# Joining the two 256-column products of a projection into one 512-column product

## The reference

```python
def swiglu(h, w_in, w_out):                       # w_in 1024 x 5632, w_out 2816 x 1024
    a, b = jnp.split(h @ w_in, 2, axis=-1)
    return (jax.nn.silu(a) * b) @ w_out

# first block, per layer: hx and hc are normalised x and ctx
q, k, v, ga, uf, gf, zc, bc, cc, gc = split_cols(hx @ w_in, PROJ_SIZES)   # 2816 columns
...                                               # the same w_in for hc; attention, Fourier, convolution
y = gated_merge(a, ga, f, gf, s, gc, w_out)       # ends in h @ w_out, 1024 x 1024

# second block, per layer: the same weights are applied to x and to hctx
x = x + 0.5 * mx[:, 2] * swiglu(ada_norm(x, ...), ffn_w_in[l, 0], ffn_w_out[l, 0])
hctx = hctx + 0.5 * mc[2] * swiglu(ada_norm(hctx, ...), ffn_w_in[l, 0], ffn_w_out[l, 0])
...                                               # mixer, then a second feed-forward network
```

## Time and profile before

| what | value |
|---|---|
| median of 3 runs (lowest, highest) | 2312.89 us (2312.33, 2319.12) |
| the profiled execution, first to last instruction | 2314.2 us |
| PE busy in it | 2227.1 us, 96% |
| DVE, ACT, POOL busy | 49%, 37%, 8% |
| mean granted PE clock | 0.987 of full speed |
| DMA, mean | 136 GB/s |

### The profile page before, as it was taken

One profiled execution on the slowest core, in us unless ns is written; L12 is line 12 of the kernel. 1 busy time (PEld: TensorE's weight loads), 2 busy tenths in 40 slices (PEclk: granted clock), 3 DMA queues, 4 the chain that ended last, 5 costly groups with the idle time before them and its releaser, 6 DMA issues. The chain is left out here.

```text
span 2314.2 us, 46991 instructions
## 1 busy us (share of the span) xinstructions
PE 2227.1 (96%) x19320; PEld 2091.2 (90%) x19320; DVE 1145.4 (49%) x1930; ACT 846.8 (37%) x1384; POOL 176.3 (8%) x150
## 2 busy tenths in 40 slices
PE   6999999899999999998999999999999999999998
PEld 5986798799999999976999999999999998979998
DVE  5227375653433445456653333454343446487665
ACT  4226454632221233248432222243232234455444
POOL 0003112100000010501200000010000010001000
PEclk9999999999999999999999999999999999999999
DMA  9853544445676244520354666242233233225573
GB/s 297 234 167 86 172 133 104 128 147 154 186 216 186 86 131 117 149 80 28 102 175 141 190 207 189 84 126 85 81 114 94 86 96 101 74 82 146 168 202 112
DMA packets 515900, 315.76 MB, mean 136 GB/s; under 512 B 16035, under 2 KB 513274, under 8 KB 515622
## 3 DMA queue, kind: packets, MB, share of 16 engines
q1 hardware_dynamic: 515160, 313.45, 46.1%
q10 hardware_dynamic: 590, 0.16, 0.0%
HBM read 312.50 MB, written 1.06 MB: 135 GB/s over the span
## 5 line engine op out<-in xcount | busy, mean ns | idle before, releaser
L1118 PE MATMUL ps<-h_hi,w_hi 128*128 128x256 f32 x3376 | 728.0, 280 | 3.5 <-DVE h_lo L1726 1.7
L1118 PE MATMUL ps<-h_lo,w_hi 128*128 128x256 f32 x3376 | 720.6, 278 | 0.0
L1118 PE MATMUL ps<-h_hi,w_lo 128*128 128x256 f32 x3376 | 720.6, 278 | 0.0
L1118 PEld LDWEIGHTS ps<-h_hi,w_hi 128*128 128x128 f32 x3376 | 537.8, 189 | 22.9 <-issue 21.6
L1118 PEld LDWEIGHTS ps<-h_lo,w_hi 128*128 128x128 f32 x3376 | 539.4, 189 | 0.1
L1118 PEld LDWEIGHTS ps<-h_hi,w_lo 128*128 128x128 f32 x3376 | 537.9, 189 | 0.0
L1960 DVE TENSOR_TENSOR w_lo<-stage,w_hi 128x1024 fp32r<-128x1024 f32 x227 | 285.0, 1258 | 441.5 <-ACT w_hi L1467 440.9
L1467 ACT ACTIVATE w_hi<-stage 128x1024 fp32r<-128x1024 f32 x227 | 236.6, 1055 | 334.4 <-PE ps L1118 200.4
L1960 DVE TENSOR_TENSOR w_lo<-deep,w_hi 128x1024 fp32r<-128x1024 f32 x184 | 226.1, 1234 | 226.9 <-ACT w_hi L1467 225.2
L1467 ACT ACTIVATE w_hi<-deep 128x1024 fp32r<-128x1024 f32 x184 | 191.9, 1055 | 179.7 <-PE ps L1118 141.4
L1118 PE MATMUL ps<-g_hi,w_hi 128*128 128x256 f32 x1100 | 232.9, 280 | 0.2
(11 more groups left out here) (413 smaller groups left out, 2858.0 us busy)
## 6 DMA issues: line engine op xcount, KB each, us to landing
modw<-in_ada_w SPq DMA_DIRECT2D x72, 1024.0 KB, 6.7
stage<-in_ffn_w_in SPq DMA_DIRECT2D x88, 512.0 KB, 3.9
deep<-in_ffn_w_in SPq DMA_DIRECT2D x88, 512.0 KB, 3.9
modw<-in_w_mod SPq DMA_DIRECT2D x18, 1024.0 KB, 6.1
stage<-in_w_in SPq DMA_DIRECT2D x30, 512.0 KB, 5.3
stage<-in_ffn_w_out SPq DMA_DIRECT2D x32, 384.0 KB, 3.5
stage<-in_even_w_in SPq DMA_DIRECT2D x24, 512.0 KB, 4.0
deep<-in_ffn_w_out SPq DMA_DIRECT2D x32, 384.0 KB, 3.4
```

Of the source, the lines that this page charges most:

```text
L1118: last = mm(ps[:, j, v - a:v - a + SEQ], w_part[wp][:, u % RING, c, :], x_part[xp][:, x, v:v + SEQ], start=first and wp == xp and v == a, ...
```

## The change

`chunk` no longer loops over the halves. Each of the three products of a chunk takes all columns `a` to `b` in one call: 512 columns where both halves of the tokens are in the projection, and 256 as before where only the latent ones are. Tiles, waits, signals and all other engines' programs stay as they are.

```diff
             def chunk(j, u, c, x, first, final):
                 for wp, xp in W_X:
-                    for v in range(a, b, SEQ):
-                        last = mm(ps[:, j, v - a:v - a + SEQ], w_part[wp][:, u % RING, c, :], x_part[xp][:, x, v:v + SEQ],
-                                  start=first and wp == xp and v == a, stop=final and wp == "lo", skip_group_check=True)
+                    last = mm(ps[:, j, 0:b - a], w_part[wp][:, u % RING, c, :], x_part[xp][:, x, a:b],
+                              start=first and wp == xp, stop=final and wp == "lo", skip_group_check=True)
                 return last
```

## The result

The changed kernel takes 2333.68 us (median of four runs, 2332.49 to 2334.57) against 2312.61 us for the kernel before on the same chip (2310.88 to 2319.12). The ratio is 1.0089, with a 95% interval from 1.0072 to 1.0106. The forecast of 2303.3 us was wrong in its sign, and the time lies outside its range. It is the time of the rival "the slow pace everywhere", 2333 us.

A forecast was written before the change was run, and what follows sets the result against it. PE's own pace was taken to bound the projections. Slow pairs saving 11 us, less 2 us for unsettled starts, plus 0.6 us for saved loads, gave 9.6 us off 2312.9: 2303.3 us, range 2297 to 2326 us.

The forecast's parts named there:

- the slow pace everywhere: Rival: unsettled 232 ns is the rule for joined products; 24 us lost, 4 gained, 2333 us; chance 0.19.
- The bound: In the projections only PE's own pace sets the end; PE is in flight for 2227.1 of 2314.2 us.
- The counts: 10788 general products of 256 columns form 5394 pairs; 5394 weight loads and 5394 starts of products go away.
- the hidden load: Weight load of 0.19 us runs beside the product before it; taking it away gives nothing by itself.
- The pace of the joined product: General products of 512 columns settle at 226.5 ns, as in the gate product; two quick halves take 226.6.
- The sum for the quick pace: About 1190 slow pairs save 11 us, unsettled starts cost 2, fewer loads at starts save 0.6: 9.6 us less.
- The mixed paces: Rival: joined products fall into quick or slow pace by stage; at 22% slow 2310 us; chance 0.23.
- The prediction's own test: Three stages of 396 products should fall from 46.96 to about 45.2 us, the 864-product projection stay at 98.
- The fixed cost per product: Rival: long projections reach 215.8 ns per 512-column product, 69 us less, 2244 us; chance 0.06.

The follow-up runs named there:

- e10: Changed kernel, weight ring moved 56 bytes on (distance 120), last network's activations 32 bytes on (distance 88): 2315.74 us, ratio 1.0010 to the kernel before.
- e9: Kernel before, still with halves of 256 columns, its weight ring moved 24 bytes on (distance 88): 2324.80 us, ratio 1.0052 to the kernel before.
- e1_streams: Small kernel of product streams alone, operand places varied from the changed kernel's addresses: 233.4 ns per 512-column product there, 226.6 with activations 64 bytes on.
- e5: Changed kernel with 192 unused bytes behind vtok, which makes the distance 0: 2324.92 us, ratio 1.0032 to the kernel before.
- e7_fine: Small kernel of product streams alone, distances in steps of 8 bytes, some 4, plus mixed kinds: 512 columns 226.7 ns at distance 120.
- e4_scan: Small kernel of product streams alone, distances 0 to 480 in steps of 32 bytes: joined products 226.6 ns at 0 and 256, 233.4 at 64.

## Why the prediction was wrong

**The bound, right.** PE's own pace sets the end, no wait grew, and the span followed the sums of the general products in each kernel of the table, up to the 5 to 10 us that everything else takes more once the layout is another.

**The counts, right; the hidden load, right at the quick pace.** 5394 products and loads went away, as counted. At their quick paces a joined product takes as long as two halves (97.98 us for 432 in e10, for 864 in e9), so that the saved loads and starts give nothing there, as the earlier trace rows let expect. Where the halves are slow, at the distances 0 and 128, joining takes 66.9 and 28.3 us off the 512-token stages; whether the load or the start that is saved does it was not separated.

**The pace of the joined product: the step that failed.** "With 128 weight columns, the very form that the change makes, ... it settles: 17 starts ..., 226.5 ns each." It is the same form only by the numbers of its shape. The gate weights lie at distance 0 from the activations, the ring at 64. The other row of 512 columns has distance 64 and 232.3 ns, and was thus the nearer one; I put its slower pace down to its 64 weight columns. e1_streams, with the place of the activations as its only change, shows 233.4 ns against 226.6 for one shape. 5394 products at 233.3 instead of 226.7 ns are 36 us. The prediction's own test named the case beforehand: 46 us or more for the stages of 198 (46.37), and 98 us that become 100 (100.95). Between the changed kernel and e10, where the weights lie 56 bytes further on, the 512-token stages differ by 1271.0 - 1236.3 = 34.7 us.

**The sum for the quick pace, right under its condition.** I had 9.6 us less for joined products that are all quick. e5 has 1247.5 - 1238.9 = 8.6 us less in those stages, e10 11.2 us. Neither kernel ended 9.6 us sooner, because in these layouts the other work of PE takes about 17 us (e5) and 8 us (e10) more (table).

**The mixed paces, not seen.** All joined products of the changed kernel have one pace; the row that was to speak for a mixture belonged to another distance.

**The rival that came true.** "The slow pace everywhere" had 24 us lost and 4 gained, 20 us more. The 512-token stages lost 23.5 us; that the median came out at 21.1 more is in part luck, since in the profiled execution the untouched latent-only stages gave 6.1 us back by a change of pace that I had only put into the range. Its reason was another too: I had put it down to products that don't settle, and it is the distance. I gave it 0.19 because 17 settled starts seemed to weigh more than 13 unsettled ones; they were not two samples of one thing.

**The fixed cost per product, excluded for these products.** No kind of 512 columns had a pace under 226.6 ns at the full clock, at any of the 39 distances of e7_fine. The 215.8 ns that follow from the rule of the Trainium skill, page "TensorE: Matmul & The Clock Gate", section "Wait — 56ns, not 53.3ns?", did not appear here.

**What stays open.** Why a distance is quick or slow. The Trainium skill, page "TensorE: Matmul & The Clock Gate", section "Step-by-step: what each phase is for", says that loading the next weights takes no read bandwidth from the running product, since PE has two read ports. These runs don't show a loss of bandwidth as such, but they do show that products with loads between them run at 226.6 to 235 ns by the layout alone. That the load and the product get into each other's way is a guess: a load of 64 columns instead of 128 took less than 1 ns off a product, and the mixed kinds of e7_fine did not fit its simple form. A product without loads beside it was not tried. Nor is it shown what chooses between the two paces of the halves at 64 and 88. The untouched last network had the other pace in the changed kernel; but one execution of each kernel was profiled, so the choice may as well differ from execution to execution. The times would fit that: 17 executions of the kernel before reach from 2309.9 to 2326.2 us, and the 12 of e5 beside them, at distance 0, where each form showed one pace only, from 2323.2 to 2327.4 us.

## What to carry to other kernels

A pace that is read from another product of the same program holds only if its operands lie the same way, so compare the addresses before you call two rows the same form. Before a change of a product's shape is judged on a kernel that PE bounds, run it at two or three layouts: here the same edit was worth +21 us, -26 us and -66 us at the distances 64, 128 and 0. And look at what the layout does to the products that the edit does not touch, since they share the ring.

## What the runs showed of the hardware

- At one granted clock (1.00), the pace of back-to-back fp32r products, each with its own load of 128 weight columns, depends on the distance of weights and activations in a partition, modulo 256 bytes: 226.6 to 235 ns for 512 columns, 113.3 to 123.4 ns for 256. The place alone changed nothing: distance 0 gave 226.7 and 226.6 ns at two places and in two banks (e1_streams), and 256 bytes more left every kind as it was (e4_scan).
- The good distances are not the same for the two forms: 0 gives the best pace at 512 columns (226.6 ns) and 120.0 ns at 256; 88 gives 113.4 ns to singles of 256 and 233.3 ns at 512.
- At some distances there are two steady paces, and a stretch keeps the one that it gets into at its start: 192 products in 22.03 or 22.52 us in two turns of one loop in e9, and 1584 products in 188.32 or 181.63 us in the kernel before and the changed one. Products of 512 columns have them at other distances: at 192, 229.0 and 233.4 ns in the two passes of e7_fine.
- The gate product needs about six products before it settles at 226.7 ns, in the kernel before and in the changed one.
